# The S5 scan of a two-block kernel: a negated sine row, 512-column additions, scans in place, and a later gated unit

## The reference, cut to what matters

```python
def s5_branch(u, a_re, a_im, log_dt, b_re, b_im, c_re, c_im, d, glu_w, glu_b):
    lam_bar = jnp.exp(lam * dt)
    b_bar = ((lam_bar - 1) / lam)[:, :, None] * b_mat
    bu = jnp.einsum('bsgh,gph->bsgp', uf.astype(jnp.complex64), b_bar)
    _, states = lax.associative_scan(combine, (a_el, bu), axis=1)   # s[t] = lam_bar * s[t-1] + bu[t]
    y = jnp.einsum('bsgp,ghp->bsgh', states, c_mat).real + d.astype(f32) * uf
    y = jax.nn.gelu(y.reshape(bsz, seq, BRANCH_W)).astype(u.dtype)
    return y * jax.nn.sigmoid(y @ glu_w + glu_b)
```

## Time and profile of the kernel before

| | |
|---|---|
| median of three executions | 1906.09 us (1905.41 to 1906.23) |
| the profiled execution: its own time, its span | 1905.72 us, 1903.7 us |
| TensorE clock granted, mean | 0.999 |
| busy, share of the span: PE, PEld, DVE, ACT, POOL | 99%, 88%, 78%, 51%, 22% |
| chain that ended last: PE, DVE, issue, ACT | 73%, 20%, 3%, 2% |
| the S5 pieces: first and last of the DVE products | 235 us, 694 us |

### The profile page before, as it was taken

How to read it: one execution, slowest core, us unless ns; L and a number is a source line. 1 busy time by engine, 2 the same in 40 slices (tenths; PEclk the granted TensorE clock), 3 DMA queues, 4 the chain that set the end, 5 groups by cost and what they waited for, 6 DMA issues and landing times.

```text
span 1903.7 us, 28439 instructions
## 1 busy us (share of the span) xinstructions
PE 1879.1 (99%) x11210; PEld 1676.6 (88%) x11210; DVE 1488.1 (78%) x2235; ACT 961.4 (51%) x1346; POOL 412.3 (22%) x310
## 2 busy tenths in 40 slices
PE   9999999999999999999999999999999999999998
PEld 8989898888878788889899988998899889989987
DVE  7977899878899986779899996777567557656755
ACT  6655554434444445548654466554345445444544
POOL 0000344424366630000397744000000000000000
PEclk9999999999999999999999999999999999999999
DMA  9766666555656666676566656666666666666664
GB/s 333 250 193 192 192 199 180 174 165 179 192 176 185 180 187 197 200 231 199 161 197 218 200 176 189 200 209 200 204 204 199 202 205 201 200 204 204 200 202 153
DMA packets 105973, 377.45 MB, mean 198 GB/s; under 512 B 11888, under 2 KB 14448, under 8 KB 105712
## 3 DMA queue, kind: packets, MB, share of 16 engines
q1 hardware_dynamic: 105552, 375.10, 64.4%
q10 hardware_dynamic: 288, 0.53, 0.1%
HBM read 372.90 MB, written 2.69 MB: 197 GB/s over the span
## 4 chain that ended last, share of the span: by engine, by line
PE 73%; DVE 20%; issue 3%; ACT 2%; DMA 1%; POOL 0%; DVEq 0%; SPq 0%; ACTq 0%
PE bank L2036 24%; PE bank L2047 12%; PE bank L2103 7%; PE bank L2101 7%; PE bank L2102 7%; DVE bank L1757 6%; DVE wl L1139 5%; PE bank L2084 3%; PE bank L2086 3%; PE bank L2085 3%; ACT wh L738 2%; DMA raw<-in_w_bxg 1%; DVE wsc L1524 1%; PE bank L2180 1%; DVE upad L1294 1%
## 5 line engine op out<-in xcount | busy, mean ns | idle before, releaser
L1139 DVE TENSOR_TENSOR wl<-raw,wh 128x1024 fp32r<-128x1024 f32 x608 | 761.0, 1257 | 319.2 <-ACT wh L738 313.7
L738 ACT ACTIVATE wh<-raw 128x1024 fp32r<-128x1024 f32 x680 | 711.0, 1053 | 542.1 <-PE bank L2103 204.9
L2036 PE MATMUL bank<-Hr,wh 128*128 128x512 f32 x1536 | 351.3, 380 | 0.5 <-DVE scrB L1188 0.5
L2036 PEld LDWEIGHTS bank<-Hr,wh 128*128 128x128 f32 x1536 | 282.4, 189 | 36.9 <-issue 0.7
L669 POOL TENSOR_TENSOR wl<-raw,wh 128x1024 fp32r<-128x1024 f32 x72 | 172.7, 2415 | 292.3 <-DVE small L1713 234.1
L2101 PE MATMUL bank<-wh,Yr 128*128 128x512 f32 x560 | 212.3, 379 | 0.0
L2102 PE MATMUL bank<-wl,Yr 128*128 128x512 f32 x560 | 212.2, 379 | 0.0
L2103 PE MATMUL bank<-wh,Yr 128*128 128x512 f32 x560 | 212.2, 379 | 0.0
L2036 PE MATMUL bank<-Yr,wh 128*128 128x512 f32 x832 | 191.3, 380 | 1.5 <-ACT wh L738 0.6
L2047 PEld LDWEIGHTS bank<-Hr,wl 128*128 128x128 f32 x1536 | 187.0, 192 | 6.3 <-issue 1.1
L2047 PE MATMUL bank<-Hr,wl 128*128 128x256 f32 x1536 | 188.3, 275 | 0.0
(11 more groups left out here) (380 smaller groups left out, 2740.2 us busy)
## 6 DMA issues: line engine op xcount, KB each, us to landing
raw<-in_w_up SPq DMA_DIRECT2D x128, 512.0 KB, 4.2
raw<-in_w_dn SPq DMA_DIRECT2D x128, 512.0 KB, 4.2
raw<-in_w_g SPq DMA_DIRECT2D x96, 512.0 KB, 3.6
raw<-in_w_p SPq DMA_DIRECT2D x80, 512.0 KB, 3.8
raw<-in_w_b SPq DMA_DIRECT2D x48, 512.0 KB, 3.6
raw<-in_w_out SPq DMA_DIRECT2D x32, 512.0 KB, 3.6
raw<-in_w_q SPq DMA_DIRECT2D x16, 512.0 KB, 4.3
raw<-in_w_av SPq DMA_DIRECT2D x16, 512.0 KB, 4.2
```

The source lines that it names most:

```text
L738: e.activation(wh[:, c % WN, :], raw[:, c % RAW, :], ACT.Copy).then_inc(s_hi, 1)
L1139: e.tensor_tensor(wl[:, c % RAW, :], raw[:, c % RAW, :], wh[:, c % WN, :].bitcast(F32), ALU.subtract).then_inc(s_low_v, 1)
L2036: ins = e.matmul(dst, wh[:, s, kk * 128:kk * 128 + 128], by_turns(pair.both[:, :, k, :]), start=i == 0 and kk == 0, stop=i == j.nch - 1 an ...
```

## The change

ScalarE writes a third row into the tables of each piece: wcs becomes cosine, minus sine, sine, in two buffers of 768 columns. With it `wm2` holds the products with minus sine and sine, and sum and difference become one addition of 512 columns, whose second operand is read with its halves swapped. The scans write where they read (`wsc` is `wm1`). The forward turn takes sine, minus sine, so that POOL's `turned` becomes one addition of 512 columns too, and the four products of `cy` for tt below 4 lie in one half of the bank, so that `s5_out` is one operation for all tt. The negation is a new ACT operation per piece, 32 in all, in step S5_AT[n - 1] + 3, behind that step's `softmax` and before its `gelu`; it waits for s_tab. DVE's second product waits for it (s_neg). In `glu` the last multiplication of tile t moves from the end of tile t to the end of tile t + 1.

```diff
-    wcs = [pair2(f"wcs{i}", o_YB + 2 * i * K1) for i in range(2)]
-    wsc = pair2("wsc", o_YB + 4 * K1)
+    wcs = [at(f"wcs{i}", o_YB + 3 * i * K1, 768).rearrange("p (r t) -> p r t", r=3) for i in range(2)]
-    wm1 = pair2("wm1", o_YB + 8 * K1)
+    wm1 = wsc = pair2("wm1", o_YB + 8 * K1)
...
         def turned(n):
             w.wait_ge(s_n, n + 1)
-            e.tensor_tensor(by_c[:, 0, :], by_c[:, 0, :], by_s[:, 1, :], ALU.subtract)
-            e.tensor_tensor(by_c[:, 1, :], by_c[:, 1, :], by_s[:, 0, :], ALU.add).then_inc(s_turned, 1)
+            e.tensor_tensor(by_c, by_c, by_s[:, ::-1, :], ALU.add).then_inc(s_turned, 1)
...
+        def negative(n):
+            w.wait_ge(s_tab, n + 1)
+            if n >= 2:
+                w.wait_ge(s_n, n - 1)
+            e.activation(wcs[n % 2][:, 1, :], wcs[n % 2][:, 2, :], ACT.Copy, scale=-1.0).then_inc(s_neg, 1)
...
             if ATT <= c < ATT + 48:
                 softmax(c)
+            if c == S5 + 1:
+                negative(0)
+            if c - 3 in S5_AT[0:31]:
+                negative(S5_AT.index(c - 3) + 1)
             if GELU <= c < GELU + 8 * GELU_STEP:
                 gelu(c)
...
-                w.wait_ge(s_glt, t + 1)
-                w.wait_ge(s_gph, t + 1)
-                e.scalar_tensor_tensor(uT[:, t, :], kept(j), 1.0, uT[:, t, :], ALU.add, ALU.mult).then_inc(s_glu, 1)
...
-            sb = wcs[n % 2][:, 1:2, :].broadcast_to((128, 2, T))
+            both_s = wcs[n % 2][:, 1:3, :]
...
+                w.wait_ge(s_n, n)
                 e.tensor_tensor(wm1, bv, cb, ALU.mult).then_inc(s_v, w.own())
-                e.tensor_tensor(wm2, bv, sb, ALU.mult).then_inc(s_m, 1)
+                w.wait_ge(s_neg, n + 1)
+                e.tensor_tensor(wm2, bv, both_s, ALU.mult).then_inc(s_m, 1)
             elif i == 2:
                 w.wait_ge(s_m, n + 1)
-                e.tensor_tensor(wm1[:, 0, :], wm1[:, 0, :], wm2[:, 1, :], ALU.add).then_inc(s_v, w.own())
-                e.tensor_tensor(wm1[:, 1, :], wm1[:, 1, :], wm2[:, 0, :], ALU.subtract).then_inc(s_v, w.own())
+                e.tensor_tensor(wm1, wm1, wm2[:, ::-1, :], ALU.add).then_inc(s_v, w.own())
...
-                e.tensor_tensor(ss, wsc, sb, ALU.mult).then_inc(s_n, 1)
+                e.tensor_tensor(ss, wsc, both_s[:, ::-1, :], ALU.mult).then_inc(s_n, 1)
...
-            if t not in S5_POOL:
-                last.then_inc(s_v, w.own())
-                w.wait_ge(s_v, w.n)
-                last = e.tensor_tensor(uT[:, t, :], uT[:, t, :], bank[6][:, T:2 * T], ALU.subtract)
...
+            j = ended(c - 1, "glu")
+            if j is not None:
+                w.wait_ge(s_glt, j.t + 1)
+                w.wait_ge(s_gph, j.t + 1)
+                e.scalar_tensor_tensor(uT[:, j.t, :], kept(j), 1.0, uT[:, j.t, :], ALU.add, ALU.mult).then_inc(s_glu, 1)
...
-                for q in range(4):
-                    e.matmul(bank[6][32 * q:32 * q + 32, T:2 * T], Cs[:, 0, 4 * tt + q, :], states(tt, q)[1][:, 1, :],
-                             start=True, stop=True)
-                for i, (r, by, part) in enumerate(((0, 0, 0), (1, 0, 1), (1, 1, 0))):
+                for i, (r, by, part) in enumerate(((0, 0, 0), (1, 0, 1), (1, 1, 0), (0, 1, 1))):
```

More of the change, by code:

```diff
@@ L555, in _build @@
     s_hm, s_hidh, s_hidl = sem("s_hm"), sem("s_hidh"), sem("s_hidl")
-    s_first, s_turned = sem("s_first"), sem("s_turned")
+    s_first, s_turned, s_neg = sem("s_first"), sem("s_turned"), sem("s_neg")
     s_tx, s_xt, s_oq, s_fin, s_fin_a = sem("s_tx"), sem("s_xt"), sem("s_oq"), sem("s_fin"), sem("s_fin_a")
@@ L684, in tables @@
             e.tensor_tensor(d[:, 0, :, :], *sides(0, 0), ALU.mult)
-            e.tensor_tensor(d[:, 1, :, :], *sides(1, 0), ALU.mult).then_inc(s_p, w.own())
+            e.tensor_tensor(d[:, 2, :, :], *sides(1, 0), ALU.mult).then_inc(s_p, w.own())
             if n >= 1:
@@ L691, in tables @@
             e.tensor_tensor(cs[:, 0, :], cs[:, 0, :], wpt[:, 1, :], ALU.subtract)
-            e.tensor_tensor(cs[:, 1, :], cs[:, 1, :], wpt[:, 0, :], ALU.add).then_inc(s_tab, 1)
+            e.tensor_tensor(cs[:, 2, :], cs[:, 2, :], wpt[:, 0, :], ALU.add).then_inc(s_tab, 1)
         def turned(n):
@@ L1514, in s5_main @@
                 w.wait_ge(s_s5, 1)
+                w.wait_ge(s_n, n)
                 e.tensor_tensor(wm1, bv, cb, ALU.mult).then_inc(s_v, w.own())
-                e.tensor_tensor(wm2, bv, sb, ALU.mult).then_inc(s_m, 1)
+                w.wait_ge(s_neg, n + 1)
+                e.tensor_tensor(wm2, bv, both_s, ALU.mult).then_inc(s_m, 1)
             elif i == 2:
                 w.wait_ge(s_m, n + 1)
-                e.tensor_tensor(wm1[:, 0, :], wm1[:, 0, :], wm2[:, 1, :], ALU.add).then_inc(s_v, w.own())
-                e.tensor_tensor(wm1[:, 1, :], wm1[:, 1, :], wm2[:, 0, :], ALU.subtract).then_inc(s_v, w.own())
+                e.tensor_tensor(wm1, wm1, wm2[:, ::-1, :], ALU.add).then_inc(s_v, w.own())
             elif i == 3:
                 rb = rr[:, k:k + 1].broadcast_to((128, T))
-                w.wait_ge(s_v, w.n - 1)
+                w.wait_ge(s_v, w.n)
                 e.tensor_tensor_scan(wsc[:, 0, :], rb, wm1[:, 0, :], 0.0, ALU.mult, ALU.add).then_inc(s_v, w.own())
-                w.wait_ge(s_v, w.n - 1)
                 e.tensor_tensor_scan(wsc[:, 1, :], rb, wm1[:, 1, :], 0.0, ALU.mult, ALU.add).then_inc(s_v, w.own())
@@ L1536, in s5_main @@
                 e.tensor_tensor(sc, wsc, cb, ALU.mult).then_inc(s_v, w.own())
-                e.tensor_tensor(ss, wsc, sb, ALU.mult).then_inc(s_n, 1)
+                e.tensor_tensor(ss, wsc, both_s[:, ::-1, :], ALU.mult).then_inc(s_n, 1)
         def s5_out(t):
             w.wait_ge(s_cy, t + 1)
-            last = e.scalar_tensor_tensor(uT[:, t, :], uT[:, t, :], cv("d", t), bank[6][:, 0:T], ALU.mult, ALU.add)
-            if t not in S5_POOL:
-                last.then_inc(s_v, w.own())
-                w.wait_ge(s_v, w.n)
-                last = e.tensor_tensor(uT[:, t, :], uT[:, t, :], bank[6][:, T:2 * T], ALU.subtract)
-            last.then_inc(s_s5y, 1)
+            e.scalar_tensor_tensor(uT[:, t, :], uT[:, t, :], cv("d", t), bank[6][:, 0:T], ALU.mult,
+                                   ALU.add).then_inc(s_s5y, 1)
         def gelu(c):
@@ L2254, in cy @@
                 w.wait_ge(s_n, 4 * tt + 4)
-                for q in range(4):
-                    e.matmul(bank[6][32 * q:32 * q + 32, T:2 * T], Cs[:, 0, 4 * tt + q, :], states(tt, q)[1][:, 1, :],
-                             start=True, stop=True)
-                for i, (r, by, part) in enumerate(((0, 0, 0), (1, 0, 1), (1, 1, 0))):
+                for i, (r, by, part) in enumerate(((0, 0, 0), (1, 0, 1), (1, 1, 0), (0, 1, 1))):
                     for q in range(4):
                         ins = e.matmul(bank[6][32 * q:32 * q + 32, 0:T], Cs[:, r, 4 * tt + q, :],
-                                       states(tt, q)[by][:, part, :], start=i == 0, stop=i == 2)
+                                       states(tt, q)[by][:, part, :], start=i == 0, stop=i == 3)
             ins.then_inc(s_cy, 1)
```

## The result

The changed kernel takes 1911.77 us (1911.26 to 1912.34) against 1906.09 us: the ratio is 1.0031, interval 1.0022 to 1.0041, so it is slower by 5.7 us. The profiled execution took 1912.34 us, the longest of seven, with a span of 1910.6 us against 1903.7.

What follows compares the result with a forecast made beforehand. From 525 to 700 us DVE's ordered list was taken as the kernel's clock, its `low`s feeding PE. Terms -1.0 - 0.4 + 0.8 - 1.0 + 1.3 + 6.2 + 0 = +5.9 gave a 1912.0 us median, range 1901.5 to 1917.0.

Steps and rivals of the forecast that it cites:

- The negation as a wait: ACT waits for POOL's `tables`, delaying `high`: 4.4 at pieces 22 to 30 plus later `tables`, +6.2 us (bounds +1 and +10).
- The +0.3 at six places: Allowance within the wait term for POOL's chain shifting and ending `tables` later: +0.3 us at each of six places.
- ACT's wait in sum: ACT's new wait for `tables`: some 40 us; DVE's idle time for `high` from 525 to 700: 3.1 to some 8.
- The merged additions: One DVE addition replaces two at twelve pieces in the busy stretch: -1.0 us, near the lower bound (bounds -1 and -8.5).
- `turned` as one addition: POOL's long addition keeps DVE from the port over four pieces in `xg`: +0.8 us (between -1 and +1.5).
- The negation as work: Four negations in `xg` stand ahead of `high` and each put ACT back by 0.32: +1.3 us.
- L1545: This `s5_out` operation of 0.42 us goes four times, only one of them in `xg` counting: -0.4 us.
- `cy(7)`: At the end of the stretch its 1.01 us wait for POOL goes, as one `turned` ends earlier: -1.0 us.
- `glu`: The moved multiplication fills DVE's first gap and lengthens the second: 0 us; +0.4 if that cover were gone.
- relief reaches PE: Rival, chance 0.17: DVE's savings shorten POOL's chain so ACT never comes late: 1901.7 us, 1897.5 with the whole bound.
- Relief and wait cancel: Rival, chance 0.25: waits cost 1 to 4 us and the additions give 2 to 3: 1903 to 1909 us, no change.
- The wait closes a loop: Rival, chance 0.06: POOL's chain grows each round, six places lose 0.74 more each, `xg` its +1.5: 1917 us.

Runs made afterwards that it cites:

- e1_late: Changed kernel with negation n moved from ACT's step S5_AT[n - 1] + 3 to S5_AT[n], one to four steps later: 1905.07 us.
- e2_before_neg: Kernel before plus only the negation and its waits, at the change's place, its result unread (three-row tables and scans in place make room): 1911.61 us.
- e9: Changed kernel, negation where the change has it, with only POOL's `turned` again as two additions of 256 columns: 1912.13 us.
- e11: e9 with DVE's merged addition also split again into two of 256 columns: 1910.34 us.
- e6_late_split: e1_late with DVE's merged addition split again into two of 256 columns: 1906.40 us.
- e3_before_copy: e2_before_neg with the ACT operation reading constants instead of the sine row, so the same work without waiting for POOL: 1906.98 us.
- e7_late_glu: e1_late with the last `glu` multiplication put back at the end of its own tile: 1905.22 us.
- e4_no_neg: Changed kernel without the negations of pieces 2 to 31, that part of the computation left out: 1904.09 us.
- e10_best: e8_later with POOL's `turned` in two additions for n < 20 and in one from 20 on: 1903.65 us.
- e8_later: Changed kernel with the negation in step S5_AT[n] + 1, one step later than in e1_late: 1904.56 us.

## Why the prediction was right, and where it was off

The forecast was 1912.0 us and the median is 1911.77; its mechanism, the wait, held. That the two lie 0.2 us apart is luck: the wait and the long addition cost 0.6 and 0.8 us more than forecast, and the profiled executions differ by 6.6 us where the medians differ by 5.7. Within the wait, the 0.98 of piece 25 did not come, and the 1.8 for a later `tables` was too small. By its steps:

- **The negation as a wait, +6.2.** The same change with the negation late (e1_late) lies 6.85 us lower from 189 to 242: 156.15 - 149.30. The place-by-place sum from the chain of before is tested best by e2_before_neg, whose additions are those of before. PE's loss there was 0.71, 0.70, 1.28 and 0.70 us at pieces 22, 26, 28 and 30, where the prediction had 0.70, 0.72, 1.28 and 0.69. The fifth, piece 25, was put at 0.98 and gave nothing: its `low`, that of chunk 211, ended 1.37 us ahead of PE. The reason is POOL's chain: in the kernel before `tables(25)` ended 10.56 us behind the product that released it, in e2_before_neg 8.63, while DVE wanted that `high` 11.03 and 11.15 us behind it. Instead 0.32 went at chunks 206 to 208, behind piece 24. The +0.3 at six places for a later `tables` had the right sign: a merge puts them back by 0.46, shown by e9 and e11, and in the changed kernel itself by 0.34 at pieces 22, 26 and 30 and 1.16 at 28.
- **ACT's wait in sum** was foretold as some 40 us and is 65.2; DVE's idle time before `low` as some 8 and is 12.7. That the total of a wait is a bad measure is shown by e1_late (21.0 us that cost nothing from 189 to 242).
- **The merged additions, -1.0.** With the negation late they are worth 1.3 us (e6_late_split). The lower bound was the right one. 13 merged additions last 0.971 on average where a stretched pair had 0.738 + 0.732 (L1520 in the same stretch), but `low` takes 1.452 on average in e1_late instead of 1.425 in e6_late_split, and 1.440 in e9_early_two instead of 1.405 in e11_early_split: POOL's turn moved there, as the prediction said.
- **`turned` as one addition, +0.8** in `xg`: mis-sized. e9_early_two, which has two, needs 84.24 where the changed kernel needs 85.88, so the long one costs 1.6 us, just past the bound of +1.5, and with the negation late 2.3 (85.90 against 83.60). It is not as long as both (1.941 us on average against 1.460 + 1.234), but DVE's `low` stands behind the whole of it. By the Trainium skill (GPSIMD Engine Reference, Performance versus the Vector engine) 512 columns were estimated at 1.3 us; the shortest in the trace take 1.28 to 1.40, so the trace agrees with that estimate for the shortest alone; the others take 2.18 to 2.87.
- **The negation as work, +1.3:** +1.2 (e3_before_copy). **L1545, -0.4:** -0.4 in `xg` (84.38 in e11_early_split, 84.80 in e2_before_neg). **`cy(7)`, -1.0:** -1.07. **`glu`, 0:** 0 (e7_late_glu).

Together: 6.85 - 1.29 (189 to 242 without the wait) + 2.31 - 1.07 = +6.8 us in the stretches of the profiled executions, where the sum of the prediction was +5.9.

Of the rivals, "relief reaches PE" is what e4_no_neg shows once the negation is away: 1.3 us from 189 to 242, near the clean saving of the merges and not the wide bound. "Relief and wait cancel" had the relief about right, but the wait cost 6.85 us and not 1 to 4. "The wait closes a loop" did not happen: POOL's chain is 8.96 us at piece 22 and 8.95 at piece 30, so its growth of 0.34 does not add up from piece to piece.

## What to carry to other kernels

An operation that is added to an engine with room costs what its semaphore makes the queue behind it wait, so its price is read from the end of what it waits for and the moment at which the next instruction behind it is wanted; here one line of placement was worth 6.7 us, more than all the rest of the change. Where the operations of two engines take turns, as those of DVE and POOL do here, count turns and not only busy time: a merged instruction gives the other engine one turn less, and a longer one holds the other up for its whole length. So a merge on the critical engine can lose, as long as something on the way to it waits for the other engine.

## What the runs showed of the hardware

In some profiled executions TensorE's clock fell at one place. PE had idled 2.09 us ahead of chunk 216, behind a `low` of 2.29 us; some 0.8 us after it had begun again, its matmuls came every 0.43 us instead of every 0.214, for 3 us (e10_best; start, duration, operation, of PE's timeline):

```profile
621.77 0.48 PE L2095 MATMUL bank<-wh,Hr 128*128 128x512 f32 x1 [2.09 <-DVE wl L1152]
...
623.04 0.63 PE L2096 MATMUL bank<-wl,Hr 128*128 128x512 f32 x1
623.47 0.63 PE L2097 MATMUL bank<-wh,Hr 128*128 128x512 f32 x1
```

In the windows of the same kernel the clock is the third figure from the end:

```profile
621.70:626.20 4.50, 4.43 (x13) 3.57 (x14) 4.50 (x6) 1.41 (x2) 4.42 (x5) 0.62 0.19 76
626.20:632.00 5.80, 5.80 (x29) 5.08 (x28) 5.80 (x7) 3.14 (x5) 1.90 (x2) 1.00 0.62 177
```

The granted clock is 0.62 on average there and 1.00 behind it; 0.43 against 0.214 is the lower of the two levels, 1.2 GHz. The changed kernel, e6_late_split and e7_late_glu show the same at that chunk, 0.7 to 1.4 us after PE had begun again. e8_later and e4_no_neg idle the same 2.09 us there and keep their clock, as the window of e8_later says:

```profile
623.00:627.50 4.50, 4.40 (x20) 3.89 (x21) 4.50 (x6) 2.48 (x3) 4.42 (x5) 1.00 0.32 96
```

In these traces it costs nothing at the end of the stretch: PE loses 1.7 us at chunk 216, but e7_late_glu, with the fall, and e1_late, without it, both need 149.30 us from 189 to 242. What e7_late_glu loses more than e1_late at chunks 214 to 217, 2.5 us, e1_late loses elsewhere: 0.9 us at 206 and 207 and 1.6 at 232 to 234. Why the clock fell in some executions and not in others stays open.
